# Rounded weights and gate activations that begin off a four-word boundary, in a transformer kernel on one NeuronCore

## The reference

```python
h = causal_dwconv(x @ w_up, conv_w, conv_b)          # up0, up1: 2048 -> 11264
gate, up = jnp.split(h, 2, axis=-1)
x = layer_norm(DN_ALPHA * x + (jax.nn.gelu(gate) * up) @ w_down, ...)   # down0, down1: 5632 -> 2048
x = x + jax.nn.sigmoid(x @ ple_w_gate[layer]) * (p[layer] @ ple_w_proj[layer])   # pg0, pg1: 2048 -> 2048
```

## Time and profile before

| | |
|---|---|
| time of the runs, median of 3 | 3286.01 us (3286.01 to 3286.4) |
| span of the profiled execution, first to last instruction | 3284.6 us |
| median of the runs less that span | 1.4 us |
| instructions | 53186 |
| PE busy (matmuls) | 3232.2 us, 98% |
| PEld busy (weight loads) | 2855.1 us, 87% |
| DVE busy | 2195.8 us, 67% |
| ACT busy | 1667.5 us, 51% |
| share of the last chain of waits on PE | 90% |
| DMA | 563.64 MB, mean 172 GB/s |

### The profile page before, as it was taken

The page is one execution under the profiler, slowest core; times in us unless marked ns, Lnnn a source line. Parts: engine busy times, 40 slices in busy tenths (PEclk is TensorE's granted clock), DMA queues, the critical chain, the costliest instruction groups (busy, mean ns, idle before and its releaser), DMA issues.

```text
span 3284.6 us, 53186 instructions
## 1 busy us (share of the span) xinstructions
PE 3232.2 (98%) x21672; PEld 2855.1 (87%) x21672; DVE 2195.8 (67%) x2836; ACT 1667.5 (51%) x2138; POOL 24.5 (1%) x38
## 2 busy tenths in 40 slices
PE   9999999999999999999999999999999999999998
PEld 8888898888888888888888888888888888888887
DVE  6577767666676456676766666745675767647676
ACT  5574346555554335554555555533564456444563
POOL 0000000000000000011000000000000000000000
PEclk9999999999999999999999999999999999999999
DMA  7352145455444554534445445455544434444342
GB/s 279 143 210 67 57 167 200 181 188 196 179 185 175 184 190 183 190 119 180 164 181 199 182 186 198 159 186 192 188 168 185 171 129 167 186 175 167 129 171 112
DMA packets 47254, 563.64 MB, mean 172 GB/s; under 512 B 5072, under 2 KB 7264, under 8 KB 10720
## 3 DMA queue, kind: packets, MB, share of 16 engines
q1 hardware_dynamic: 47072, 561.06, 45.4%
HBM read 558.92 MB, written 2.12 MB: 171 GB/s over the span
## 4 chain that ended last, share of the span: by engine, by line
PE 90%; DVE 5%; ACT 3%; issue 2%; DMA 0%; SPq 0%; DVEq 0%; ACTq 0%
PE bank L863 40%; PE bank L849 21%; PE bank L968 10%; PE bank L973 5%; PE bank L1002 3%; ACT spl_r L1771 1%; PE bank L1468 1%; DVE ring L2506 1%; PE bank L784 1%; PE bank L788 1%; PE bank L782 1%; DVE spl_r L2506 1%; DVE xb L2506 1%; DVE xa L2506 0%; DVE scr L2506 0%
## 5 line engine op out<-in xcount | busy, mean ns | idle before, releaser
L2506 DVE TENSOR_TENSOR spl_r<-ring,spl_r 128x2048 fp32r<-128x2048 f32 (+2 forms) x429 | 961.3, 2242 | 485.8 <-ACT spl_r L1771 480.8
L863 PE MATMUL bank<-all_r,spl_r 128*128 128x512 f32 x4960 | 1196.6, 393 | 3.2 <-ACT spl_r L1771 3.2
L1771 ACT ACTIVATE spl_r<-ring 128x2048 fp32r<-128x2048 f32 x407 | 779.2, 1915 | 591.0 <-PE bank L849 484.1
L863 PEld LDWEIGHTS bank<-all_r,spl_r 128*128 128x128 f32 x4960 | 914.5, 188 | 189.5 <-issue 8.0
L849 PEld LDWEIGHTS bank<-all_r,spl_r 128*128 128x128 f32 x5008 | 642.1, 191 | 24.2
L849 PE MATMUL bank<-all_r,spl_r 128*128 128x256 f32 x5008 | 650.0, 283 | 0.0
L2506 DVE TENSOR_TENSOR dsp_r<-ring,dsp_r 128x1408 fp32r<-128x1408 f32 x126 | 204.8, 1625 | 206.4 <-ACT dsp_r L1771 206.2
L968 PE MATMUL bank<-scr_r,dsp_r 128*128 128x512 f32 x1386 | 338.8, 392 | 0.0
L1771 ACT ACTIVATE dsp_r<-ring 128x1408 fp32r<-128x1408 f32 x126 | 174.4, 1384 | 283.3 <-PE bank L973 283.1
L968 PEld LDWEIGHTS bank<-scr_r,dsp_r 128*128 128x128 f32 x1386 | 252.5, 189 | 47.4
L863 PE MATMUL bank<-scr_r,spl_r 128*128 128x512 f32 x1152 | 275.8, 391 | 2.9 <-ACT spl_r L1771 2.9
(11 more groups left out here) (437 smaller groups left out, 2673.9 us busy)
## 6 DMA issues: line engine op xcount, KB each, us to landing
ring<-in_up SPq DMA_DIRECT2D x88, 2048.0 KB, 7.8
ring<-in_down SPq DMA_DIRECT2D x64, 1408.0 KB, 6.0
ring<-in_ib SPq DMA_DIRECT2D x34, 2048.0 KB, 7.8
ring<-in_pg SPq DMA_DIRECT2D x16, 2048.0 KB, 7.8
ring<-in_out SPq DMA_DIRECT2D x16, 2048.0 KB, 7.9
ring<-in_in SPq DMA_DIRECT2D x12, 2048.0 KB, 7.7
ring<-in_ec SPq DMA_DIRECT2D x11, 2048.0 KB, 8.4
ring<-in_ea SPq DMA_DIRECT2D x8, 2048.0 KB, 10.5
```

What stands on the lines that cost most here:

```text
L863: mm(b[:, :], WHI[half][:, kk, :], pair(name, kk), start=kk == 0, stop=False, skip_group_check=True)
L1771: A(high[half], w[:, :, half * P:(half + 1) * P], ACT.Copy).then_inc(S["w_hi"], count)
L2506: return V.tensor_tensor(out, a, b, op)
```

## The change

Every buffer of rounded weights in `spl_r` begins one word later, every one in `dsp_r` three words later. The rounded activations of `pg0` begin one word later and those of `pg1` three words later, both parts, so the step between them stays. The arena grows by eight words. Two things move along because they are placed by `SPL`: a block of plain weights that is loaded by one DMA (`LG`) and a buffer of the scan stage (`BF`); `DOWN_FIRST`, the first piece of the down product, shifts by one word, not three. `rstd` moves by eight words. The second half of the first weights of `up0` and `up1` (`FIRST_SECOND_HALF`) stays where it was, and so do all other activations. Every engine has the same instructions in the same order with the same waits and the same sizes; only start addresses differ.

```diff
-SPL = 19456
+SPL = 19456 + 1
-SCR = 2 * (HHW + FC * 2 * P) - 2 * T
+SCR = 2 * (HHW + FC * 2 * P) - 2 * T + 8
+SHIFTS = {"pg0": 1, "pg1": 3}
...
-        scr_r, spl_r = named("scr_r", 2 * X, 2 * HHW, FR), named("spl_r", 2 * X + SPL, 8192, FR)
-
-        dsp_r = named("dsp_r", 2 * X + 2 * HHW, 4 * FC * P, FR)
+        scr_r, spl_r = named("scr_r", 2 * X, 2 * HHW, FR), named("spl_r", 2 * X + SPL - 1, 8200, FR)
+
+        dsp_r = named("dsp_r", 2 * X + 2 * HHW, 4 * FC * P + 8, FR)
...
-        all_r = named("all_r", 0, 2 * X + SCR, FR)
+        all_r = named("all_r", 0, 2 * X + SCR - 8, FR)
...
-        WHI, WLO = ([spl_r[:, 4096 * h + o:4096 * h + o + 2048].rearrange("p (k n) -> p k n", n=P)
+        WHI, WLO = ([spl_r[:, 1 + 4096 * h + o:1 + 4096 * h + o + 2048].rearrange("p (k n) -> p k n", n=P)
                      for h in range(2)] for o in (0, 2048))
 
-        DHI, DLO = ([dsp_r[:, FC * P * (2 * h + o):FC * P * (2 * h + o + 1)].rearrange("p (k n) -> p k n", n=P)
+        DHI, DLO = ([dsp_r[:, 3 + FC * P * (2 * h + o):3 + FC * P * (2 * h + o + 1)].rearrange("p (k n) -> p k n", n=P)
                      for h in range(2)] for o in range(2))
...
-                    "pg0": (xav, rtiles(scr_r, 5632), rtiles(scr_r, 9728)),
+                    "pg0": (xav, rtiles(scr_r, 5632 + SHIFTS["pg0"]), rtiles(scr_r, 9728 + SHIFTS["pg0"])),
                     "od_out": (QQ, rtiles(scr_r, 6144), rtiles(scr_r, 10240)),
-                    "pg1": (xbv, rtiles(scr_r, 5632), rtiles(scr_r, 9728))})
+                    "pg1": (xbv, rtiles(scr_r, 5632 + SHIFTS["pg1"]), rtiles(scr_r, 9728 + SHIFTS["pg1"]))})
...
-                return scrv[:, a:b + 1:b - a, :]
+                shift = SHIFTS.get(name, 0)
+                shifted = scr_r[:, shift:shift + 80 * T].rearrange("p (a t) -> p a t", t=T)
+                return shifted[:, a:b + 1:b - a, :]
```

## The result

| | before | changed |
|---|---|---|
| median of the runs | 3286.01 us (3285.45 to 3286.4, 4 runs) | 3297.95 us (3297.01 to 3302.45, 4 runs) |
| span of the profiled execution | 3284.6 us | 3300.7 us |
| mean granted clock in it | 0.997 | 0.995 |

The ratio is 1.0039, with a 95% interval of 1.0023 to 1.0055 (the two medians alone give 1.0036). "No change within 0.2%" was forecast; the kernel is slower. The medians lie 11.9 us apart; the two profiled executions lie 16.1 apart, because the one of the changed kernel was the longest of its four runs, 3302.45 us.

What follows compares the result with a forecast made beforehand. PE's stream of matmuls at its own pace was taken to bound the kernel. All terms were 0 on the span of 3284.6 us; with the median 1.4 us above it, 3286 us was forecast, range 3277 to 3440 us.

Steps and rivals of the forecast that it cites:

- No change within 0.2%: Whole kernel: the addresses move but every stage keeps its pace, 3286 us; chance 0.52.
- PE's pace bounds the kernel, and DVE, ACT and the DMA don't matter.: Whole kernel: TensorE is busy 98% of the span; odd words for DVE, ACT and DMA were each taken as 0.
- PE loads weights from odd words: I take 0.: Matmuls with shifted weights: no cost taken, between 212 us gained and 1013 plus 90 us lost.
- The rival of the collision: Weights and activations stop colliding at the start: up to 13.3 ns a matmul faster, 212 us, 3074 us; chance 0.12.
- The rival of the odd moving stream: pg0 and pg1 alone: moving operand from odd words is slower, up to 151 us for both, 3437 us; chance 0.14.
- The rival of the odd weight block: 256-column matmuls: slower weight load, 8 to 32 us (chance 0.12) or far more, to 1103 us (0.04).

Runs made afterwards that it cites:

- e6: Against the changed kernel: weights 8 words on, 16 in down, gate activations 8 in pg0 and 0 in pg1; 3304.46 us beside 3286.91 before.
- e9: Kernel before, no shifts, but pg0's moving operand is one word reread and pg1's weight block one word reread, in regular halves; 3284.22 us beside 3286.41.
- e1: Changed kernel with the gate activations of pg0 and pg1 back at their old place, weights still shifted; 3295.83 us, ratio to before 1.0027.
- e2: Changed kernel with all weights back at their old place, only gate activations shifted, 1 in pg0 and 3 in pg1; 3289.39 us, ratio 1.0006.
- e4: Changed kernel with shifts exchanged: weights 3 words on, 1 in down; gate activations 3 in pg0, 1 in pg1; 3290.85 us, ratio 1.0010.
- e10: Against the changed kernel: all weights two words on, gate activations unshifted; 3273.9 us beside 3286.41 before, ratio 0.9963.
- e3: Against the changed kernel: all weights and pg0's activations four words on, pg1's activations unshifted; 3283.76 us beside 3287.37 before.

## Why the prediction was wrong

- *PE's pace bounds the kernel, and DVE, ACT and the DMA don't matter.* Right. The splits took 2294, 1626 and 1916 ns, PE's waits did not grow, and the loss is in PE's pace.
- *PE loads weights from odd words: I take 0.* This is the step that failed: the term measured +4.2 ns on 512 columns and -1.6 on 256 at one word, +0.3 and -1.5 at three, some 12 of the 15 us of the sum above. I drew it from two kinds of rows. The DVE tap was right about DVE and says nothing of PE. The rows of plain matmuls beside `mat` and the ring seemed to show that the place has no influence in steps of eight words; but they were taken on a form that shows next to none of the excess (429 ns for 512 columns, which I myself set against 426.7), and e6 shows that eight words cost an fp32r product 4.6 ns on 512 columns. And the equal paces of the earlier trace rows stand at distances that are all multiples of 128 words, so by the period of 64 words they are one place, not three. Three equal rows were one observation.
- *The rival of the collision* came nearest to the mechanism, two reads of PE that depend on each other's place, and had only one direction of it. It took the excess of 15 and 13 ns for what a shift can take away. The shift moved the two kinds in opposite directions: +4.2 and -1.6 ns. At one word the loss on 512 columns wins, at two the gain on 256. What the walking stream pays in full is 12.4 and 8.0 ns by e9; on all of them that would be 12.4 x 7498 + 8.0 x 8442 = 160 us of the kernel, an estimate, against my bound of 212. My reason against it, that the excess looks like a price of the fp32r form because plain matmuls have none, fell with e9: the same form goes at 216.0 ns when its stream stands still.
- *The rival of the odd moving stream* was right in kind for pg0, and small: 7.3 ns on 512 columns and 4.3 on 256 over e1, 2.6 us in its 448 regular matmuls, where my bound was half of 151. For pg1, three words on, it was wrong: 1.4 ns less on 512 columns.
- *The rival of the odd weight block* was wrong: it priced the 256-column matmuls, whose weight loads seemed to set the pace, and these became faster. The measured time lies in its 8 to 32 us, and in my range of 3277 to 3440 us, by luck: in the sum behind those 8 to 32 us the 512-column matmuls, which are the ones that lost, have no price.

The Trainium skill, "TensorE: Matmul & The Clock Gate", in "Step-by-step: what each phase is for", says that loading the next weights takes no SBUF read bandwidth from the running matmul, PE having two independent read ports; "SBUF — State Buffer", "Who interferes with whom", says that PE waits for nobody. By this rule no distance could matter and the forecast would have held. The runs, all on fp32r, disagree: 228.4 ns fall to 216.0 when the moving stream stands still, and the place of the weights alone moves the pace between 226.7 and 233.3 ns. The floor that the first page gives for back-to-back matmuls under "Wait — 56ns, not 53.3ns?", 215.7 ns for 512 columns, agrees with those 216.0.

Open are: why two rhythms exist at 3, 4, 12 and 60 words (and with both operands at 66), and what picks one; what is special about a start at word 1; and what has a period of 64 words. All places but those of the changed kernel, e1, e2, e4 and e10 were run once.

## What to carry to other kernels

Where PE is busy throughout with fp32r matmuls that each load their own weights, as here, the distance of weights from activations is a free parameter worth some tenths of a per cent, and should be swept on the chip, not reasoned out; here two words gave 0.37%, and 63 words, the worst, cost 0.9% in one run. Buffers of round sizes all put their operands at the same distance, so equal paces in many stages are no evidence that the place is indifferent. Before a pace is taken as a floor, let one stream stand still in one stage and see what is left.

## What the runs showed of the hardware that I had not expected

- fp32r matmuls, each with its own weight load: 228.4 ns for 512 columns and 119.5 for 256 in the kernel before; with a moving operand of one word 216.0 and 111.5. Once a row has settled, the kernel before pays the same 13.3 ns over 213.3 and 106.7 on both kinds (steps of 226.6 and 120.0 ns).
- The pace depends on the distance of the two operands and repeats after 64 words: 64 like 0 (229.2 / 119.3 in down), 66 like 2 (230.6 / 115.7), 32 not like 0 (232.7 / 118.6).
- The same addresses gave 226.7 and 233.2 ns on 512 columns in different stages of one execution (e3), each constant over a whole stage after its first row.
- The price of the place needs no other engine: with ACT, DVE and DMA idle at the end of out21, the 256-column steps are 119.5 ns before and 117.9 changed, as in up0 with both at work.
- Long runs that start at an odd word cost neither DVE (2294 against 2292 ns) nor ACT (1916 against 1915) anything.
